# Pool caches handed over transposed, and a 64-token sample tile in retention

## The chip, the cores and the metric

The kernel runs on one core of a Trainium2 chip. The metric is the device time of one execution in microseconds (us), lower is better. TensorE is called PE below, VectorE DVE, ScalarE ACT, GpSimd POOL and SyncE SP.

## The reference

Two layers, each a mixer and a mixture of experts, on 512 prompt tokens and a sample group of 8 sequences with 8 new tokens each (64 tokens). All data is float32.

```
u, q, k, v, g = split(rmsnorm(x) @ w_in)                    # 512 columns each
pool: c = cumsum(concat([prev, u]))                         # prev: cache_pool, the last 15 rows of u of each sample sequence
      d = (c[t] - c[t - w]) / w - u                         # w = 2, 4, 8, 16 for the four groups of 128 channels
      y = d @ w_pool[group] * pool_scale
retention (4 heads of 128), in chunks:
      scores = (q @ k.T) * decay_mat
      o      = scores @ v + (q * q_decay) @ s
      o      = (o - mean(o)) * rsqrt(var(o) + eps);  ret_out = silu(g) * o
x += concat([pool_out, ret_out]) @ w_out
x += HierMoE(rmsnorm(x))                                    # 16 experts, two for each token
```

For the prompt the chunk is 128 tokens with a carried state; for the samples it is the 8 tokens of a sequence, with the state `state_ret` of that sequence.

## The kernel before

**Tiles of tokens.** Tokens lie in five tiles (`NT = 5`): tiles 0 to 3 are the prompt, the last (`LAST = 4`) holds the 64 sample tokens (`NSAMP`) in its first 64 rows. `tokens(t)` is 128 for a prompt tile and 64 for the last.

**Large products.** Each float32 product is made of float32r matmuls of a high and a low part of both factors (lines L464 to L468, 512 columns each): ACT makes the high part of a 256 KB piece of weights (`wh`), DVE the low part (`wl`), SP loads the pieces into `raw`. The input product runs over 40 such steps (`WIN_STEPS`: five groups of 512 columns, eight steps each), the output product over 16 more (`wout_mm`).

**What is put between the steps.** The order on every engine is written out by hand. After some input steps PE does a piece of pooling or retention: at steps `U_AT = (9, 13, 17, 21)` it turns `u` of one channel group so that channels are on partitions (five transposes of a 128x128 tile, L1744 and L1745), and with a sixth (L1746) the pool caches of the samples, `cpn`, 120 rows of which (8 sequences of 15) were loaded token by token. ACT copies the three pieces into `uT` (`pool_u`, L1175 to L1177), POOL adds shifted copies of it (`window`, L842), DVE makes `dT` (`pool_d`, L2187 to L2193), and PE multiplies it by `wpool` (`pool_mix`, L1364) at steps `M_AT = (12, 16, 20, 25)`. POOL also does the rotary embedding (`rotate`, L822 to L825) between the windows.

**Retention.** For each tile `qk_t` transposes q and k, `scores` multiplies them (L1630), DVE multiplies the result by the decay (`score_decay`, L2235) into `scT`, and `outputs` (L1645, L1647, L1651) makes the outputs and the state of prompt tiles. The last tile goes through `scores` too, but its outputs are made by `sample_head`, transposed: a matmul of v with `scT` (L1663) and, for each sequence, one of its state with its 8 queries (L1665). ACT copies these four heads into `scT[1]`, `back` transposes them (L1696), and from there the last tile is treated as the others: `group_stats`, `group_root`, `group_norm`, `gated`, and `on_t`, which transposes the normed outputs for the output product (L1373). `sample_head`, `back` and `on_t` stand between steps of the output product.

**Then** come the router, a gather of the tokens of each expert by indirect DMA (L857, `hg<-xn_d,rowidx`), 16 experts, a scatter and the sums, and the next layer. `idle_turns` (L1410) are matmuls of zeros that only keep PE busy.

Of the kernel before, what the change touches and what calls it, by code (L numbers as in the profile page):

```python
# [18 lines left out]
ALU = mybir.AluOpType  # L19
ACT = mybir.ActivationFunctionType  # L20
# [7 lines left out]
P = 128  # L28
D = 1024
SEQ, DECB, DECS, PAST = 512, 8, 8, 4096  # L30
NL = 2
# [99 lines left out]
def build(nc, a, o):  # L131
# [6 lines left out]
    with ctx:  # L138
# [9 lines left out]
        def tile(name, shape, dt=F32, off=None):  # L148
            size = int(np.prod(shape[1:])) * (2 if dt == BF16 else 4)
            return nc.alloc_sbuf_tensor_at(name, shape, dt, offset=place(size) if off is None else off)  # L150
# [7 lines left out]
        pscale = tile("pscale", [P, NH])  # L158
        gn_at = place(4096)
        gnrow = tile("gnrow", [P, PW], off=gn_at)  # L160
        cpn = tile("cpn", [DECB * BUF, PW], off=gn_at + 2048)
        wr = tile("wr", [P, KC, 20])
        gcol = tile("gcol", [P, 2, NL, KC])
        rbias = tile("rbias", [P, 20])
# [199 lines left out]
        def c(name, *shape):  # L364
            v = cst[:, at[name][0]:at[name][1]]
            if len(shape) == 1:
                return v.rearrange("p (a b) -> p a b", a=shape[0])
            if len(shape) == 2:
                return v.rearrange("p (a b c) -> p a b c", a=shape[0], b=shape[1])
            return v  # L370
# [6 lines left out]
        def zq(t, name):  # L377
            return z[:, t, OFFS[name], :]

        def heads(ap):  # L380
            return ap.rearrange("p (h d) -> p h d", h=NH)
# [22 lines left out]
        def tokens(t):  # L404
            return NSAMP if t == LAST else P
# [178 lines left out]
        def _(sp):  # L584
# [60 lines left out]
            def pool_tables(L):  # L645
                if L:
                    sp.wait_ge(comb, COMBS * L)
                sp.dma_start(cpn[:, :], a["cache_pool"][L].rearrange("b r c -> (b r) c")).then_inc(small_ld, 16)
                sp.dma_start(wpool[:, :, :], a["w_pool"][L]).then_inc(small_ld, 16)
                sp.dma_start(pscale[:, :], a["pool_scale"][L]).then_inc(small_ld, 16)  # L650

# [316 lines left out]
        def _(sc):  # L968
# [200 lines left out]
            def pool_u(L, g):  # L1169

                if g or L:
                    sc.wait_ge(d_done, NH * L + g)
                sc.wait_ge(ut_done, NH * L + g + 1)
                samp = uT[:, 16 + SEQ:].rearrange("p (b w) -> p b w", b=DECB)
                sc.activation(uT[:, 16:16 + SEQ], ps[6][:, :], ACT.Copy).then_inc(uT_done, 1)  # L1175
                sc.activation(samp[:, :, 16:24], ps[7][:, 0:NSAMP].rearrange("p (b s) -> p b s", b=DECB), ACT.Copy).then_inc(uT_done, 1)
                sc.activation(samp[:, :, 1:16], ps[7][:, P:P + DECB * BUF].rearrange("p (b s) -> p b s", b=DECB), ACT.Copy).then_inc(uT_done, 1)  # L1177

            def pool_hi(L, g):

# [24 lines left out]

            def group_root(L, t):
                sc.wait_ge(gn_st, NT * L + t + 1)
                sc.activation(gnrt[:, :], mv[:, :, 1], ACT.Sqrt, bias=eps[:, 1:2], scale=1.0).then_inc(gn_rt, 1)

            def first_hi(k):  # L1210
                raw_there(sc, 0, k)
# [5 lines left out]
            for L in range(NL):  # L1217
# [50 lines left out]
                sc.wait_ge(st_ready, LAST * (L + 1))  # L1268
                sc.dma_start(o["new_ret_prompt"][L], st[:, :, :]).then_inc(st_st, 16)
                sc.wait_ge(o_mm, NT * (L + 1))  # L1270
                sc.activation(scT[1][:, :, :], heads(ps[B_OT][:, :]), ACT.Copy).then_inc(o_ev, 1)
                w_hi(L, WIN_STEPS + 8)
                o_hi(sc, L, 0)
                o_hi(sc, L, 1)
# [92 lines left out]
        def on_t(pe, L, t):  # L1367

            pe.wait_ge(on_done, NT * L + t + 1)
            if t >= 2:  # L1370
                pe.wait_ge(olo, NT * L + t - 1)
            for h in range(NH):
                last = pe.transpose(ps[B_ON[t % 2]][:, h * P:(h + 1) * P], on[t][:, h, :], ident)  # L1373
            last.then_inc(on_tr, 1)

# [1 line left out]
        def _(pe):  # L1378
# [245 lines left out]
            def scores(L, t):  # L1624

                T = NT * L + t
                pe.wait_ge(qk_ev, 2 * T + 2)
                pe.wait_ge(qd_done, T + 1)
                for h in range(NH):
                    last = pe.matmul(ps[B_SC][:, h * P:(h + 1) * P], kT[:, h, :], qT[:, h, :], start=True, stop=True)  # L1630
                last.then_inc(sc_mm, 1)

            def outputs(L, t):
# [20 lines left out]
            def sample_head(L, h):  # L1654

                if h == 0:
                    pe.wait_ge(sc_ev, NT * (L + 1))
                    pe.wait_ge(kd_done, NT * (L + 1))
                    for t in (2, 3, LAST):
                        z_there(pe, L, 4, t)  # L1660
                pe.wait_ge(s0_ld[h], 16 * (L + 1))
                out = ps[B_OT][:, h * P:(h + 1) * P]
                pe.matmul(out, zq(LAST, "v")[:, h * P:(h + 1) * P], scT[0][:, h, :], start=True, stop=False)  # L1663
                for b in range(DECB):
                    last = pe.matmul(out[:, b * DECS:(b + 1) * DECS], s0[h][:, b, :], qdT[0][:, h, b * DECS:(b + 1) * DECS],  # L1665
                                     start=False, stop=(b == DECB - 1))
                if h == NH - 1:
                    last.then_inc(o_mm, 1)
# [23 lines left out]
            def back(L):  # L1692

                pe.wait_ge(o_ev, L + 1)
                for h in range(NH):
                    last = pe.transpose(ps[B_OT][:, h * P:(h + 1) * P], scT[1][:, h, :], ident)  # L1696
                last.then_inc(o_back, 1)

            def own_rows(t):
# [16 lines left out]
            for L in range(NL):  # L1716
# [12 lines left out]
                for s in range(EARLY[L], WIN_STEPS):  # L1729
                    if L == 0 and s < KC:  # L1730
                        first_block(s)
                    else:
                        for t in range(NT):
                            win_mm(L, s, t)
                    if s in U_AT:
                        g = U_AT.index(s)
                        if g == 0:
                            for t in range(NT):
                                z_there(pe, L, 0, t)
                            pe.wait_ge(small_ld, 96 * L + 64)  # L1740
                        else:
                            pe.wait_ge(plo, 8 * L + 2 * g)
                        for t in range(LAST):
                            pe.transpose(ps[6][:, t * P:(t + 1) * P], unat[:, t, g * P:(g + 1) * P], ident)  # L1744
                        pe.transpose(ps[7][:, 0:P], unat[:, LAST, g * P:(g + 1) * P], ident)  # L1745
                        pe.transpose(ps[7][:, P:P + DECB * BUF], cpn[:, g * P:(g + 1) * P], ident[0:DECB * BUF, 0:DECB * BUF]).then_inc(ut_done, 1)  # L1746
                    if s in M_AT:
                        pool_mix(pe, L, M_AT.index(s))
                    if s in T_AT:
                        qk_t(L, T_AT.index(s))  # L1750
                    if s in S_AT:
                        scores(L, S_AT.index(s))
                    if s in O_AT:
                        outputs(L, O_AT.index(s))
# [235 lines left out]
        def _(ve):  # L1990
            chain = [0]

            def link(ins):

                chain[0] += 1
                ins.then_inc(dve_chain, 1)
                ve.wait_ge(dve_chain, chain[0])
# [233 lines left out]
            def score_decay(L, t):  # L2231

                T = NT * L + t
                ve.wait_ge(sc_mm, T + 1)
                ve.tensor_tensor(scT[t % 2][:, :, :], heads(ps[B_SC][:, :]), c("decay", 2, NH)[:, int(t == LAST), :, :], ALU.mult).then_inc(sc_ev, 1)  # L2235

            def o_bank(t):
                return ps[B_O if t < LAST else B_OT]

            def group_stats(L, t):  # L2240

                if t < LAST:
                    ve.wait_ge(o_mm, NT * L + t + 1)
                else:
                    ve.wait_ge(o_back, L + 1)
                for h in range(NH):
                    last = ve.bn_stats(bnst[:, h, :], o_bank(t)[:, h * P:(h + 1) * P])
                link(last)
                for h in range(NH):
                    last = ve.bn_aggr(mv[:, h, :], bnst[:, h, :])  # L2250
                last.then_inc(gn_st, 1)

            def state(L, t):
# [13 lines left out]
            def group_norm(L, t):  # L2267

                T = NT * L + t
                ve.wait_ge(gn_rt, T + 1)  # L2270
                link(ve.reciprocal(gnrs[:, :], gnrt[:, :]))
                for h in range(NH):
                    last = ve.tensor_scalar(on[t][:, h, :], o_bank(t)[:, h * P:(h + 1) * P], mv[:, h, 0:1], gnrs[:, h:h + 1], ALU.subtract, ALU.mult)
                last.then_inc(gn_free, 1)

            def gated(L, t):

                T = NT * L + t
                ve.wait_ge(gn_free, T + 1)
                ve.wait_ge(sg_done, T + 1)  # L2280
                ve.tensor_tensor(on[t][:, :, :], on[t][:, :, :], heads(zq(t, "g")), ALU.mult).then_inc(on_done, 1)

            def sample_state(L, h):

# [189 lines left out]
```

## Time and profile before

| | |
|---|---|
| median of 3 runs | 837.12 us (836.44 to 838.64) |
| the profiled execution | 837.1 us, its span 835.1 us |
| busy share of the span | PE 97%, PE weight loads 79%, DVE 72%, ACT 58%, POOL 38% |
| mean granted clock of TensorE | 0.995 |

The span runs from the first to the last instruction. Times inside the span count from its start: layer 0 has its mixer up to about 235 us and its experts up to 400, layer 1 its mixer up to 646 and its experts up to 810. A busy PE is not a PE at its peak, so the rows are read by when the next instruction starts, and not by how long one lasts.

### The profile page before, as it was taken

The numbers are of one execution on the slowest core, as the hardware profiler recorded it, in microseconds if no ns is written. First come the engines' busy times: TensorE is split into PE (matmuls) and PEld (weight loads), VectorE is DVE, ScalarE is ACT, GpSimd is POOL, SyncE is SP. The second block draws the span as 40 slices with busy tenths as digits, with TensorE's granted clock in tenths as the row PEclk, the third lists the DMA queues.
The fourth block names the chain that finished last, engine by engine and source line by source line (L and its number), as shares of the span: only waits on it lengthen the run. The fifth ranks groups of instructions, "written<-read, shape, count | busy, mean of one in ns | idle before, by whom it ended". The sixth has DMA issues, their size and how long they took to land.

```text
span 835.1 us, 11973 instructions
## 1 busy us (share of the span) xinstructions
PE 814.2 (97%) x4104; PEld 656.6 (79%) x4104; DVE 599.4 (72%) x957; ACT 483.6 (58%) x824; POOL 315.4 (38%) x205
## 2 busy tenths in 40 slices
PE   9999999999999999999899999999999999999994
PEld 6887788888867888888488788888878578888861
DVE  5444654645689999999744454656647899999986
ACT  5533342612478888887653433353333898888874
POOL 0016991301041345664100199803101423665540
PEclk9999999999999999999999999999999999999998
DMA  9832223223939999998753222322278599999968
GB/s 323 271 109 76 72 57 98 91 70 137 411 128 361 388 355 377 397 368 300 255 185 92 85 76 64 87 64 78 78 263 346 179 417 360 383 378 391 344 219 280
DMA packets 57422, 188.17 MB, mean 225 GB/s; under 512 B 10877, under 2 KB 11645, under 8 KB 49163
## 3 DMA queue, kind: packets, MB, share of 16 engines
q1 hardware_dynamic: 44314, 156.55, 52.2%
q0 software_dynamic: 10368, 23.09, 7.4%
q10 hardware_dynamic: 2688, 7.88, 2.5%
q8 instruction: 29, 0.48, 0.2%
q14 instruction: 23, 0.18, 0.1%
HBM read 173.00 MB, written 29.39 MB: 242 GB/s over the span
## 4 chain that ended last, share of the span: by engine, by line
PE 71%; DVE 16%; DMA 5%; issue 4%; ACT 2%; DVEq 0%; ACTq 0%; POOLq 0%
PE ps L464 14%; PE ps L468 11%; PE ps L467 11%; PE ps L1414 5%; PE ps L1416 5%; PE ps L1415 5%; DVE gul L2110 4%; DVE dnl L2115 3%; PE ps L466 3%; PE ps L1422 2%; DVE hgTl L2126 2%; DMA y_d<-y,rowidx 2%; PE ps L1665 2%; DMA back<-y_d 1%; PE ps L1605 1%
## 5 line engine op out<-in xcount | busy, mean ns | idle before, releaser
L464 PE MATMUL ps<-wh,hT 128*128 128x512 f32 x472 | 189.4, 401 | 0.8 <-DVE wl L2101 0.4
L866 POOL DMA_INDIRECT y_d<-y,rowidx x32 | 116.4, 3638 | 124.1 <-DVE y L2135 124.1
L2110 DVE TENSOR_TENSOR gul<-wgu,eh 128x1024 fp32r<-128x1024 f32 x128 | 150.4, 1215 | 0.5 <-ACT eh L1105 0.5
L468 PE MATMUL ps<-wh,lT 128*128 128x512 f32 x377 | 147.2, 390 | 0.0
L467 PE MATMUL ps<-wl,hT 128*128 128x512 f32 x377 | 147.0, 390 | 0.0
L1105 ACT ACTIVATE eh<-wgu 128x1024 fp32r<-128x1024 f32 x128 | 128.4, 1058 | 3.7 <-PE ps L1416 3.7
L2101 DVE SCALAR_TENSOR_TENSOR wl<-raw,gcol,wh 128x512 fp32r<-128x512 f32 x80 | 75.3, 946 | 67.9 <-ACT wh L1078 67.8
L464 PEld LDWEIGHTS ps<-wh,hT 128*128 128x128 f32 x472 | 88.8, 188 | 18.8 <-issue 1.7
L1414 PE MATMUL ps<-eh,hgTh 128*128 128x512 f32 x240 | 96.4, 401 | 0.4 <-issue 0.4
L1416 PE MATMUL ps<-eh,hgTl 128*128 128x512 f32 x240 | 93.8, 391 | 0.0
L1415 PE MATMUL ps<-gul,hgTh 128*128 128x512 f32 x240 | 93.5, 390 | 0.0
L1078 ACT ACTIVATE wh<-raw,gcol 128x512 fp32r<-128x512 f32 x80 | 57.5, 721 | 57.9 <-PE ps L466 53.2
L468 PEld LDWEIGHTS ps<-wh,lT 128*128 128x128 f32 x377 | 70.8, 188 | 15.2
L467 PEld LDWEIGHTS ps<-wl,hT 128*128 128x128 f32 x377 | 71.0, 188 | 12.9
L2115 DVE TENSOR_TENSOR dnl<-wdn,eh 128x1024 fp32r<-128x1024 f32 x64 | 75.3, 1214 | 1.8 <-ACT eh L1118 1.7
L1118 ACT ACTIVATE eh<-wdn 128x1024 fp32r<-128x1024 f32 x64 | 64.5, 1061 | 0.0
L842 POOL TENSOR_TENSOR winA<-uT 128x719 f32<-128x719 f32 x8 | 11.1, 1387 | 115.3 <-ACT uT L1177 115.1
L857 POOL DMA_INDIRECT hg<-xn_d,rowidx x32 | 37.9, 1184 | 44.0 <-PE ps L1422 35.1
L1416 PEld LDWEIGHTS ps<-eh,hgTl 128*128 128x128 f32 x240 | 45.0, 188 | 9.9
L1414 PEld LDWEIGHTS ps<-eh,hgTh 128*128 128x128 f32 x240 | 45.1, 188 | 9.2 <-issue 0.8
L1415 PEld LDWEIGHTS ps<-gul,hgTh 128*128 128x128 f32 x240 | 45.2, 188 | 8.5
L1414 PE MATMUL ps<-eh,actTh 128*128 128x512 f32 x120 | 49.5, 413 | 0.0
(259 smaller groups left out, 1555.6 us busy)
## 6 DMA issues: line engine op xcount, KB each, us to landing
wgu<-in_gate_up SPq DMA_DIRECT2D x64, 1024.0 KB, 12.6
wdn<-in_w_down SPq DMA_DIRECT2D x64, 512.0 KB, 12.2
raw<-in_w_in SPq DMA_DIRECT2D x79, 256.0 KB, 2.7
raw<-in_w_out SPq DMA_DIRECT2D x32, 256.0 KB, 3.0
back<-y_d SPq DMA_DIRECT2D x16, 512.0 KB, 5.9
s<-in_state_ret POOLq DMA_DIRECT2D x8, 512.0 KB, 4.3
xn_d<-xf ACTq DMA_DIRECT2D x8, 512.0 KB, 6.2
x_in<-in_x_cols SPq DMA_DIRECT2D x8, 288.0 KB, 5.0
```

The lines of the kernel that those rows point to most:

```text
L464: pe.matmul(out, both, w_h, start=first, stop=False)
L467: pe.matmul(out, both, w_l, start=False, stop=False)
L468: return pe.matmul(out, l[:, t * P:(t + 1) * P], w_h, start=False, stop=final)
L866: pool.indirect_dma_start(out=y_d, out_offset=bass.IndirectOffsetOnAxis(ap=rowidx[:, 1, e:e + 1], axis=0), in_=y[s][:, :], in_offset=None, ...
L1105: sc.activation(gu_split(e, p)[:, :], gu_pair(wgu, wgu3, e, s, p), ACT.Copy).then_inc(ghi, 1)
L1118: sc.activation(dn_split(e, k)[:, :], dn_chunk(wdn, wdn3, e, s, k), ACT.Copy).then_inc(dhi, 1)
L1414: pe.matmul(out, hi_l, hi_r, start=first, stop=False)
L1415: pe.matmul(out, hi_l, lo_r, start=False, stop=False)
L1416: return pe.matmul(out, lo_l, hi_r, start=False, stop=final)
L2101: ve.scalar_tensor_tensor(out=wl[S % SPL][:, :], in0=raw[S % RAW][:, :], scalar=gcol[:, 0, L, s % KC:s % KC + 1], in1=wh[S % SPL][:, :].bi ...
L2110: ve.tensor_tensor(gu_pair(gul, gul3, e, s, p), gu_pair(wgu, wgu3, e, s, p), gu_split(e, p)[:, :].bitcast(F32), ALU.subtract).then_inc(glo, 1)
L2115: ve.tensor_tensor(dn_chunk(dnl, dnl3, e, s, k), dn_chunk(wdn, wdn3, e, s, k), dn_split(e, k)[:, :].bitcast(F32), ALU.subtract).then_inc(d ...
```

## The change

The host lays the pool caches out as channel, group, row (`pool_cols`), and SP loads them into `cpT` in place of `cpn`. PE no longer transposes them; ACT copies them from `cpT` to `uT`, ahead of the two copies that wait for PE's transposes. The wait for the small tables (`small_ld`) moves from PE to ACT, save for the first on PE. For the last tile, scores, decay, outputs, statistics, norm, gate and both transposes are cut to 64 tokens.

```diff
-        cpn = tile("cpn", [DECB * BUF, PW], off=gn_at + 2048)
+        cpT = tile("cpT", [P, NH, DECB * BUF], off=gn_at + 2048)
...
-                sp.dma_start(cpn[:, :], a["cache_pool"][L].rearrange("b r c -> (b r) c")).then_inc(small_ld, 16)
+                sp.dma_start(cpT[:, :, :], a["pool_cols"][L]).then_inc(small_ld, 16)
...
                 if g or L:
                     sc.wait_ge(d_done, NH * L + g)
+                samp = uT[:, 16 + SEQ:].rearrange("p (b w) -> p b w", b=DECB)
+                sc.wait_ge(small_ld, 96 * L + 64)
+                sc.activation(samp[:, :, 1:16], cpT[:, g, :].rearrange("p (b s) -> p b s", b=DECB), ACT.Copy).then_inc(uT_done, 1)
                 sc.wait_ge(ut_done, NH * L + g + 1)
-                samp = uT[:, 16 + SEQ:].rearrange("p (b w) -> p b w", b=DECB)
                 sc.activation(uT[:, 16:16 + SEQ], ps[6][:, :], ACT.Copy).then_inc(uT_done, 1)
                 sc.activation(samp[:, :, 16:24], ps[7][:, 0:NSAMP].rearrange("p (b s) -> p b s", b=DECB), ACT.Copy).then_inc(uT_done, 1)
-                sc.activation(samp[:, :, 1:16], ps[7][:, P:P + DECB * BUF].rearrange("p (b s) -> p b s", b=DECB), ACT.Copy).then_inc(uT_done, 1)
...
-                sc.activation(scT[1][:, :, :], heads(ps[B_OT][:, :]), ACT.Copy).then_inc(o_ev, 1)
+                sc.activation(scT[1][:, :, 0:NSAMP], heads(ps[B_OT][:, :])[:, :, 0:NSAMP], ACT.Copy).then_inc(o_ev, 1)
...
+            n = tokens(t)
             for h in range(NH):
-                last = pe.transpose(ps[B_ON[t % 2]][:, h * P:(h + 1) * P], on[t][:, h, :], ident)
+                last = pe.transpose(ps[B_ON[t % 2]][:, h * P:h * P + n], on[t][0:n, h, :], ident[0:n, 0:n])
             last.then_inc(on_tr, 1)
...
+                n = tokens(t)
                 for h in range(NH):
-                    last = pe.matmul(ps[B_SC][:, h * P:(h + 1) * P], kT[:, h, :], qT[:, h, :], start=True, stop=True)
+                    last = pe.matmul(ps[B_SC][0:n, h * P:h * P + n], kT[:, h, 0:n], qT[:, h, 0:n], start=True, stop=True)
                 last.then_inc(sc_mm, 1)
...
-                out = ps[B_OT][:, h * P:(h + 1) * P]
-                pe.matmul(out, zq(LAST, "v")[:, h * P:(h + 1) * P], scT[0][:, h, :], start=True, stop=False)
+                out = ps[B_OT][:, h * P:h * P + NSAMP]
+                pe.matmul(out, zq(LAST, "v")[0:NSAMP, h * P:(h + 1) * P], scT[0][0:NSAMP, h, 0:NSAMP], start=True, stop=False)
...
-                    last = pe.transpose(ps[B_OT][:, h * P:(h + 1) * P], scT[1][:, h, :], ident)
+                    last = pe.transpose(ps[B_OT][0:NSAMP, h * P:(h + 1) * P], scT[1][:, h, 0:NSAMP], ident)
...
-                            pe.wait_ge(small_ld, 96 * L + 64)
+                            if L == 0:
+                                pe.wait_ge(small_ld, 64)
...
-                        pe.transpose(ps[7][:, 0:P], unat[:, LAST, g * P:(g + 1) * P], ident)
-                        pe.transpose(ps[7][:, P:P + DECB * BUF], cpn[:, g * P:(g + 1) * P], ident[0:DECB * BUF, 0:DECB * BUF]).then_inc(ut_done, 1)
+                        pe.transpose(ps[7][:, 0:P], unat[:, LAST, g * P:(g + 1) * P], ident).then_inc(ut_done, 1)
...
-                ve.tensor_tensor(scT[t % 2][:, :, :], heads(ps[B_SC][:, :]), c("decay", 2, NH)[:, int(t == LAST), :, :], ALU.mult).then_inc(sc_ev, 1)
+                n = tokens(t)
+                ve.tensor_tensor(scT[t % 2][0:n, :, 0:n], heads(ps[B_SC][:, :])[0:n, :, 0:n], c("decay", 2, NH)[0:n, int(t == LAST), :, 0:n],
+                                 ALU.mult).then_inc(sc_ev, 1)
...
-                ve.tensor_tensor(on[t][:, :, :], on[t][:, :, :], heads(zq(t, "g")), ALU.mult).then_inc(on_done, 1)
+                n = tokens(t)
+                ve.tensor_tensor(on[t][0:n, :, :], on[t][0:n, :, :], heads(zq(t, "g"))[0:n], ALU.mult).then_inc(on_done, 1)
...
+    caches = host["cache_pool"].reshape(NL, DECB * BUF, NH, P)
+    host["pool_cols"] = np.ascontiguousarray(caches.transpose(0, 3, 2, 1))
```

`group_stats`, `group_root` and `group_norm` are cut to the first 64 partitions in the same way; their instructions keep their number and their 128 elements in each partition.

On PE, after step 9 of the input product of layer 0 (and the same at the other seven places in `U_AT`), these rows stand; `cst` is the identity:

```order
 L464 MATMUL ps<-wh_61,hT 128x512
 L466 MATMUL ps<-wl_65,hT 128x512
-L1744 MATMUL ps<-cst,unat 128x128 x4
-L1745 MATMUL ps<-cst,unat 128x128
-L1746 MATMUL ps<-cst,cpn 128x120
+L1749 MATMUL ps<-cst,unat 128x128 x4
+L1750 MATMUL ps<-cst,unat 128x128
 L464 MATMUL ps<-wh_62,hT 128x512
 L467 MATMUL ps<-wl_66,hT 128x512
```

One of six transposes is gone; nothing else moves.

On ACT, at the first `pool_u` of layer 0, between steps of weights:

```order
 L1078 ACTIVATE wh_60<-raw_82,gcol 128x512 [waits wpe,raw_ld0]
-L1175 ACTIVATE uT<-ps 128x512 [waits ut_done]
-L1176 ACTIVATE uT<-ps 128x8x8
-L1177 ACTIVATE uT<-ps 128x8x15
+L1175 ACTIVATE uT<-cpT 128x8x15 [waits small_ld]
+L1177 ACTIVATE uT<-ps 128x512 [waits ut_done]
+L1178 ACTIVATE uT<-ps 128x8x8
 L1078 ACTIVATE wh_61<-raw_83,gcol 128x512 [waits wpe,raw_ld1]
```

The copy of the caches has moved ahead of the wait for PE, and two copies in place of three stand behind it.

On PE, the transposes of the normed outputs of the last tile (`on_211`), between steps 7 and 8 of the output product of layer 0:

```order
 L464 MATMUL ps<-wh_63,hP 128x512
 L466 MATMUL ps<-wl_67,hP 128x512
-L1373 MATMUL ps<-cst,on_211 128x128 x4
+L1376 MATMUL ps<-cst,on_211 128x64 x4
 L464 MATMUL ps<-wh_60,hT 128x512
 L467 MATMUL ps<-wl_64,hT 128x512
```

Their number and place stay; each has half the columns (the shape is that of the output). The same holds for the other narrowed matmuls.

## Rows read from the trace of the kernel before

**Rows 1.** The page: busy time, and the chain that ended last

```profile
PE 814.2 (97%) x4104; PEld 656.6 (79%) x4104; DVE 599.4 (72%) x957; ACT 483.6 (58%) x824; POOL 315.4 (38%) x205
...
PE 71%; DVE 16%; DMA 5%; issue 4%; ACT 2%; DVEq 0%; ACTq 0%; POOLq 0%
```

**Rows 2.** Waits of PE: total us, times, longest us

```profile
PE ps L1393 <- DVE x L2220: 2.1, 2, 1.6
...
PE ps L1364 <- DVE dT L2193: 0.2, 1, 0.2
```

**Rows 3.** Busy time by stretches: us, PE, PEld, DVE, ACT, POOL, clock, DMA

```profile
97.00:211.00 114.00, 114.00 (x637) 98.56 (x636) 60.67 (x145) 41.27 (x83) 42.14 (x38) 1.00 0.30 97
...
429.00:640.00 211.00, 210.20 (x1097) 176.92 (x1095) 112.35 (x222) 83.10 (x170) 74.64 (x61) 1.00 0.36 121
```

**Rows 4.** Weight loads by form: busy us, mean ns

```profile
L1630 PEld LDWEIGHTS ps<-qT,kT 128*128 128x128 f32 x80 | 10.5, 191 | 0.8
...
L1373 PEld LDWEIGHTS ps<-cst,on 128*128 128x128 f32 x40 | 4.7, 140 | 0.5
...
L1689 PEld LDWEIGHTS ps<-vb,kv_end 64*128 64x128 f32 x16 | 2.7, 186 | 4.9 <-issue 4.2 <-DVE y L2135 0.6
L1605 PEld LDWEIGHTS ps<-wr,xT 128*64 128x64 f32 x32 | 2.3, 141 | 0.7 <-issue 0.5
```

**Rows 5.** Timeline of weight loads after step 9: start us, us

```profile
38.68 0.14 PEld L1745 LDWEIGHTS ps<-cst,unat 128*128 128x128 f32 x1
38.79 0.14 PEld L1746 LDWEIGHTS ps<-cst,cpn 120*128 120x128 f32 x1
38.90 0.19 PEld L464 LDWEIGHTS ps<-wh,hT 128*128 128x128 f32 x1
```

**Rows 6.** Timeline of PE, the scores of the last tile, layer 0

```profile
162.29 1.06 PE L1630 MATMUL ps<-qT,kT 128*128 128x128 f32 x8
163.18 0.39 PE L1645 MATMUL ps<-z,scT 128*128 128x128 f32 x2
```

**Rows 7.** Timeline of weight loads, router logits of the last tile

```profile
235.30 0.54 PEld L1605 LDWEIGHTS ps<-wr,xT 128*64 128x64 f32 x8 [0.23 <-issue]
```

**Rows 8.** Timeline of PE at a pool product

```profile
48.59 1.02 PE L1364 MATMUL ps<-dT,wpool 128*128 128x512 f32 x2
49.45 0.33 PE L1365 MATMUL ps<-dT,wpool 128*128 128x64 f32 x2
```

**Rows 9.** Timeline of PE in `sample_head`, head 1

```profile
173.38 0.38 PE L1663 MATMUL ps<-scT,z 128*128 128x128 f32 x2
173.60 1.85 PE L1665 MATMUL ps<-qdT,s 128*128 128x8 f32 x16
175.31 0.48 PE L464 MATMUL ps<-wh,hP 128*128 128x512 f32 x1
```

**Rows 10.** Timeline of ACT at `pool_u`, group 3 of layer 0

```profile
82.86 0.60 ACT L1175 ACTIVATE uT<-ps 128x512 f32<-128x512 f32 x1 [2.42 <-PE ps L1746]
...
83.45 0.28 ACT L1177 ACTIVATE uT<-ps 128x120 f32<-128x120 f32 x1
```

**Rows 11.** Timelines of DVE, POOL and PE at that group's product

```profile
91.24 1.26 DVE L2187 TENSOR_TENSOR edge<-winB,cst 128x16 f32<-128x16 f32 x1
...
90.84 1.63 POOL L822 TENSOR_TENSOR ropA<-z,cst 128x512 f32<-128x512 f32 x1
...
95.10 0.39 PE L466 MATMUL ps<-wl,hT 128*128 128x512 f32 x1
95.71 1.12 PE L1364 MATMUL ps<-dT,wpool 128*128 128x512 f32 x2 [0.23 <-DVE dT L2193]
```

**Rows 12.** Stretch of layer 0 at half the clock, columns as rows 3

```profile
236.40:239.80 3.40, 3.40 (x18) 1.59 (x17) 2.40 (x11) 2.69 (x5) 2.16 (x3) 0.50 0.35 77
```

**Rows 13.** The chain from a first transpose to the gather, both layers

```profile
226.88 0.92 PE ps L1393 x8
...
243.38 4.41 DMA hg<-xn_d,rowidx
...
637.62 0.92 PE ps L1393 x8
...
653.33 4.43 DMA hg<-xn_d,rowidx
```

More of the change, by code:

```diff
@@ L1207, in group_root @@
                 sc.wait_ge(gn_st, NT * L + t + 1)
-                sc.activation(gnrt[:, :], mv[:, :, 1], ACT.Sqrt, bias=eps[:, 1:2], scale=1.0).then_inc(gn_rt, 1)
+                n = tokens(t)
+                sc.activation(gnrt[0:n, :], mv[0:n, :, 1], ACT.Sqrt, bias=eps[0:n, 1:2], scale=1.0).then_inc(gn_rt, 1)
             def first_hi(k):
@@ L2245, in group_stats @@
                     ve.wait_ge(o_back, L + 1)
+                n = tokens(t)
                 for h in range(NH):
-                    last = ve.bn_stats(bnst[:, h, :], o_bank(t)[:, h * P:(h + 1) * P])
+                    last = ve.bn_stats(bnst[0:n, h, :], o_bank(t)[0:n, h * P:(h + 1) * P])
                 link(last)
                 for h in range(NH):
-                    last = ve.bn_aggr(mv[:, h, :], bnst[:, h, :])
+                    last = ve.bn_aggr(mv[0:n, h, :], bnst[0:n, h, :])
                 last.then_inc(gn_st, 1)
@@ L2270, in group_norm @@
                 ve.wait_ge(gn_rt, T + 1)
-                link(ve.reciprocal(gnrs[:, :], gnrt[:, :]))
+                n = tokens(t)
+                link(ve.reciprocal(gnrs[0:n, :], gnrt[0:n, :]))
                 for h in range(NH):
-                    last = ve.tensor_scalar(on[t][:, h, :], o_bank(t)[:, h * P:(h + 1) * P], mv[:, h, 0:1], gnrs[:, h:h + 1], ALU.subtract, ALU.mult)
+                    last = ve.tensor_scalar(on[t][0:n, h, :], o_bank(t)[0:n, h * P:(h + 1) * P], mv[0:n, h, 0:1], gnrs[0:n, h:h + 1],
+                                            ALU.subtract, ALU.mult)
                 last.then_inc(gn_free, 1)
@@ L2280, in gated @@
                 ve.wait_ge(sg_done, T + 1)
-                ve.tensor_tensor(on[t][:, :, :], on[t][:, :, :], heads(zq(t, "g")), ALU.mult).then_inc(on_done, 1)
+                n = tokens(t)
+                ve.tensor_tensor(on[t][0:n, :, :], on[t][0:n, :, :], heads(zq(t, "g"))[0:n], ALU.mult).then_inc(on_done, 1)
             def sample_state(L, h):
```

## The prediction

> **What bounds the kernel now.** I read the page first: PE is busy 97% of the span and holds 71% of the chain that ended last, DVE 16% [rows 1]. The list of PE's waits comes next, since busy time is no proof: the longest entry is 2.1 us in all, at the start of layer 1, and the only one inside a mixer's middle part is 0.2 us before a pool product [rows 2]. Then the stretches of the mixers: from 97 to 211 us PE is busy 114.00 of 114.00 us, from 429 to 640 us 210.20 of 211.00, at the full clock, while DVE, ACT and POOL are idle about half the time or more and DMA is at 0.30 and 0.36 [rows 3]. So in the mixer each thing that PE does adds its own slot to the time, and a slot is the distance between starts, since neighbours overlap. Everything that the change removes or narrows on PE lies in these two mixers, so a slot saved should reach the end, if no other engine is late by as little as the slot.
>
> **What a slot costs.** Two things can set it, the load of the weights and the streaming of the other tile. Streaming: a pass of 512 float32 columns takes (49.45 - 48.59) / 2 = 0.43 us [rows 8], which is 0.84 ns a column, so 128 columns are 107 ns and 64 are 54. Weights of an ordinary float32 matmul: the 16 passes that stream only 8 columns still stand (175.31 - 173.60) / 16 = 107 ns apart [rows 9], so a load of 128 columns holds the array for at least 107 ns whatever is streamed. With 64 columns of weights, 8 loads last 0.54 us together, one alone 0.141: (0.54 - 0.14) / 7 = 57 ns each [rows 4, 7]. A load lasts 191 ns with 128 columns and 141 with 64 [rows 4]. In a transpose the load of a full 128 columns lasts 140 ns [rows 4], as long as the half-width ordinary one, so I take it to hold the array for only some 57 ns; the transposes' slot of 109 ns (38.79 to 38.90) [rows 5] then comes from streaming the identity.
>
> **The change, part by part.**
>
> The cache transposes: eight are removed, four in a layer, at 109 ns from one load to the next [rows 5]. 8 x 0.109 = 0.87 us. This is the surest term; each stands alone in a dense row of PE.
>
> The scores of the last tile: 4 matmuls, 8 passes, in each layer, (163.18 - 162.29) / 8 = 111 ns a pass [rows 6]. Weights and stream are both halved: 57 ns by the load, 54 by the stream, so 57. 16 x 0.054 = 0.86 us.
>
> `on_t` of the last tile: 8 transposes. Weights stay 128 columns wide (64 rows), the identity shrinks to 64 columns: from 109 to about 57 ns, 8 x 0.052 = 0.42 us. The price hangs on the reading of the 140 ns load. Bounds: 0 if the load were the limit after all, 0.44 if streaming alone counted (8 x 0.055).
>
> `back`: 8 transposes whose weights shrink to 64 columns while the whole identity is streamed, 107 ns as before. I take 0; the upper bound is 8 x 0.052 = 0.42 us.
>
> The v matmul of `sample_head`: 8 matmuls, 16 passes; the stream shrinks to 64 columns, the weights keep 128 columns and lose only rows. The passes of 8 columns beside them stand at 107 ns [rows 9], and a load with 64 rows and 128 columns lasts 186 ns against 191 with 128 rows [rows 4]. I take 0; the upper bound is 16 x 0.054 = 0.86 us.
>
> [...]
>
> ACT: the copy of the caches (0.28 us) moves ahead of the wait for PE. ACT stands idle 2.42 us there [rows 10], so the copy lies in idle time, and `uT` is complete about 0.1 us (copy) + 0.11 us (transpose) sooner. If that cover were gone the copy would cost 0.28 us eight times on ACT, which itself is idle half of the mixer, so nothing on PE. The wait for `small_ld` that ACT takes over cannot be later than before: PE made the same wait ahead of the transposes that ACT then waited for. What is queued behind it on ACT is the next high part of weights, with the same bound.
>
> DVE and ACT on the narrower tile: `score_decay` and the copy of the outputs lose half their elements, the others none; PE waits for neither [rows 2], so 0. The cache load has as many bytes for the same issue, so 0.
>
> What is late next: the one place where DVE holds PE up is the pool product of group 3 in layer 0, which starts 95.71 - 95.10 = 0.61 us after its forerunner instead of 0.23 us. There DVE's 16-element `edge` lasts 1.26 us, up to the end of POOL's `ropA` (90.84 + 1.63 = 92.47) [rows 11]. POOL's start and DVE's start both move with PE's, so I leave this wait as it is; 0.38 us could be won there.
>
> Sum: 0.87 + 0.86 + 0.42 = 2.15 us. The profiled execution took 837.1 us (835.1 us of span and 2.0 around it), the median of the runs is 837.12. 837.1 - 2.1 = **835.0 us**, 0.25% less. A measurement of this kernel can tell some 0.3% (2.5 us) from no change, so the likeliest case is just inside "no difference".
>
> **The rivals.**
>
> *Less is paid back* (836.1 us, 0.17). The weight load bounds transposes and half-width scores gain less: 0.87 us and little more arrives, 1.0 us in all. [...] Against it: the 57 ns loads. It too is "no difference".
>
> *All narrowing pays* (833.7 us, 0.13). `back` and `sample_head` gain as well: 2.15 + 0.42 + 0.86 = 3.4 us. Against it: the 107 ns of the 8-column passes.
>
> *The clock no longer falls before the experts* (834.2 us, 0.18). In layer 0 the granted clock is 0.50 (1.2 GHz) from 236.4 to 239.8 [rows 12], after PE has done short transposes and logits; in layer 1 the same work leaves it at 2.4 GHz. From the same transposes to the first gather layer 0 takes 243.38 - 226.88 = 16.50 us and layer 1 653.33 - 637.62 = 15.71 [rows 13]: the fall costs 0.8 us. The change brings this place 1.1 us forward in layer 0 and 2.1 in layer 1, so the fall may go (835.0 - 0.8 = 834.2), or come in layer 1 too (835.8, which is in the likeliest case's range).
>
> *POOL and DVE meet worse* (slower, 841 us, 0.06). `edge` shows that a short DVE operation can stand for the whole of a POOL operation. `uT` comes a little sooner in relation to DVE, so POOL's windows and rotations shift against `pool_d`. If each of its four operations for group 3 waited out one more POOL operation of 1.63 us, that is 6.5 us in a layer, of which PE would feel nearly all in layer 0, and most in layer 1. That gives 835.0 + 6 = 841. It decides once the added stall passes 2.1 + 2.5 = 4.6 us over both layers. Against it: the shift is only some 0.1 us, and groups 0 to 2 never held PE. [...]
>
> *The change does what it says, but elsewhere* is no case of its own: both mixers are bound by PE.
>
> **How the numbers follow.** The likeliest case, 2.15 us with 0.4 either way for the terms and 0.8 for the clock, has 0.46 (834.2 to 836.0). Faster by over 0.3%: all narrowing and the lost clock fall, with a little of the likeliest, 0.13 + 0.18 + 0.03 = 0.34. Slower: 0.05 of the POOL case. Within 0.3%: 0.61. The range of 8 in 10 takes in all narrowing at its low end with a little of the clock, and no gain at its upper end, since the runs shown differ by 2.2 us: 833.0 to 837.0.
>
> **What would show it.** In the profile after: five transposes of `unat` at each of the eight places, and L464 right behind them; the 8 score passes of the last tile about 57 ns apart (0.45 us in place of 0.89); `on_t` of the last tile about 57 ns apart; `back` still near 108; the v passes of `sample_head` still near 110. The distance from the first pool transposes to the first logits should shrink by 1.07 us in each layer. The prediction is wrong if `on_t` stays at 109, if v passes fall to 57, if PE's waits before the pool products grow from 0.2 us, or if the stretch at 0.50 goes or doubles.

## The result, and the profile after

The changed kernel took 848.07 us (median of 6 runs, 844.59 to 851.20) against 836.78 us (6 runs, 835.88 to 839.19) of the kernel before: a ratio of 1.0133, with a 95% interval of 1.0118 to 1.0149. It is slower by 11 us, where 2 us less had been forecast. Its runs also lie further apart, 6.6 us against 3.3 us.

The page of the changed kernel, busy time, the granted clock in 40 slices and the chain that ended last, as in [rows 1]:

```profile
PE 827.3 (98%) x4096; PEld 662.0 (78%) x4096; DVE 600.1 (71%) x957; ACT 483.3 (57%) x824; POOL 315.5 (37%) x205
...
PEclk9999999989999999999999999999699999999998
...
PE 71%; DVE 17%; DMA 5%; issue 4%; ACT 2%; DVEq 0%; POOLq 0%; ACTq 0%
```

PE has eight instructions fewer and is busy 13 us longer. The busy time of DVE, ACT and POOL differs by less than 1 us. The row of the clock says where to look: it has a dent at slice 9 (170 to 191 us) and a deep one at slice 29 (594 to 615 us). The waits of PE do not explain 11 us; this is their first row, and the row of the pool product that answers to [rows 2]:

```profile
PE ps L1396 <- DVE x L2224: 2.2, 2, 1.6
...
PE ps L1366 <- DVE dT L2197: 0.6, 2, 0.3
```

The stretches of the changed kernel around the dents (columns as in [rows 3]; the eighth column is the granted clock, 1.00 for full speed and 0.50 for half of it):

```profile
177.20:180.60 3.40, 3.40 (x24) 2.85 (x24) 3.26 (x5) 1.05 (x3) 0.00 (x0) 1.00 0.43 143
180.60:184.00 3.40, 3.40 (x10) 2.65 (x9) 1.90 (x3) 0.63 (x1) 0.00 (x0) 0.50 0.66 181
184.00:187.50 3.50, 3.50 (x25) 2.95 (x24) 0.00 (x0) 0.22 (x1) 0.00 (x0) 0.99 0.17 60
187.50:190.90 3.40, 3.40 (x10) 2.63 (x9) 0.69 (x1) 0.69 (x2) 0.00 (x0) 0.51 0.19 64
...
586.80:590.20 3.40, 3.40 (x10) 2.36 (x8) 0.00 (x0) 0.00 (x0) 0.00 (x0) 0.50 0.00 0
...
593.60:603.90 10.30, 10.30 (x34) 8.38 (x33) 5.16 (x8) 2.19 (x4) 0.00 (x0) 0.50 0.40 127
...
607.30:610.70 3.40, 3.40 (x9) 2.66 (x9) 0.69 (x1) 0.82 (x2) 0.00 (x0) 0.50 0.18 55
```

PE is "busy" all the time in each of them. The stretch from 180.60 to 184.00, at 0.50, holds large matmuls alone, 10 of them; at the full clock's 0.23 us apiece it would be 14 or 15. (The 24 and 25 of the stretches at full clock have the 18 short passes of a head in them.) In the mixers of this execution the clock is at 0.50 for 3.4 + 3.4 us in layer 0 and 3.4 + 10.2 + 3.4 us in layer 1, 24 us in all. I call each such stretch a fall. The kernel before has 1.00 from 97 to 211 and from 429 to 640 [rows 3].

The loss arises where the falls are. Matched matmul by matmul with the kernel before, the output product's matmul that started at 155.8 us starts 0.1 us earlier in the changed kernel, the one of 195.8 us starts 4.4 us later; in layer 1 it is 4.4 us at 566.6 and 13.6 us at 606.5. Between the two pairs lie the four heads of `sample_head` of each layer.

The timeline of PE in the changed kernel shows what stands right before a fall, and how the large matmuls slow down in it:

```profile
177.47 0.39 PE L466 MATMUL ps<-wl,hP 128*128 128x512 f32 x1
177.79 0.43 PE L1667 MATMUL ps<-scT,z 64*128 64x64 f32 x2
178.16 1.95 PE L1669 MATMUL ps<-qdT,s 128*128 128x8 f32 x16
179.96 0.48 PE L464 MATMUL ps<-wh,hP 128*128 128x512 f32 x1
...
181.25 0.63 PE L467 MATMUL ps<-wl,hP 128*128 128x512 f32 x1
181.68 0.63 PE L468 MATMUL ps<-wh,lP 128*128 128x512 f32 x1
```

A head of `sample_head` precedes the fall, as it does each of the other four, and from 181.25 the large matmuls start 0.43 us apart, where it was 0.23. The head itself has become longer: from L466 to L464 it is 179.96 - 177.47 = 2.49 us, against 0.23 + (175.31 - 173.38) = 2.16 us before [rows 9]. The v product, now 64*128, starts 0.32 us after the matmul ahead of it instead of 0.23, and its two passes last to 178.16, 0.37 us, instead of 0.22, although each streams half as many columns. The weight loads at the head ahead of that one show what is different, first in the kernel before and then in the changed one:

```profile
172.93 0.19 PEld L468 LDWEIGHTS ps<-wh,lP 128*128 128x128 f32 x1
173.16 0.41 PEld L1663 LDWEIGHTS ps<-scT,z 128*128 128x128 f32 x2
...
173.06 0.19 PEld L468 LDWEIGHTS ps<-wh,lP 128*128 128x128 f32 x1
173.60 0.29 PEld L1667 LDWEIGHTS ps<-scT,z 64*128 64x128 f32 x2 [0.35 <-issue]
173.97 0.63 PEld L1669 LDWEIGHTS ps<-qdT,s 128*128 128x128 f32 x5
```

The load of 128 rows began 0.23 us after the load ahead of it, 0.22 us before its own matmul (173.38 [rows 9]). The load of 64 rows begins 0.54 us after the load ahead of it and only 0.01 us before its own matmul starts (173.61): it is not done under the running matmul any more. The full load behind it, at 173.97, starts together with its own matmul too. "issue" says that the engine waited for nothing that the profile shows; why the load isn't made earlier, no run here shows.

For each group of small matmuls I took the distance from the start of the large matmul ahead of it to the start of the second large one behind it, where both are at the full clock, in both traces (ns; groups as in the source):

```
group                               times   before   after   difference
u and cache transposes                8      1120     1011      -108
scores, last tile (with outputs 3)    2      4040     3942       -98
sample_head, one head                 8      2466     2802      +336
back and on_t 0, 1                    2      1771     1771         0
on_t, last tile                       2       900     1046      +146
pool product, group 3, layer 0        1      2031     2108       +77
pool product, group 3, layer 1        1      1548     2115      +567
```

The sum is -0.86 - 0.20 + 2.69 + 0 + 0.29 + 0.64 = +2.6 us before any fall of the clock. (Of the eight heads five are read at the full clock and differ by 335 to 336; the 336 is taken for the other three.) The profiled executions are 850.35 - 837.1 = 13.3 us apart, which leaves 10.7 us. The falls account for it: in 24 us at half the clock large matmuls stand 0.43 us apart and not 0.23, which loses 24 x (1 - 0.23 / 0.43) = 11.2 us; the fall at 236 us, 0.8 us in the prediction's reckoning, is missing in this execution, where the clock is 1.00 from 229 to 247. What is left, some 0.3 us, is no more than what arises between the layers (0.6 us). The six runs bear it out: the mean granted clock sinks from 0.989 in the fastest (844.59 us) to 0.981 in the slowest (851.20), with 0.983 and 0.985 between.

### The profile page after: what moved, and what is told of

Read it like the earlier page. It is cut to its first block, busy times and chain, and to the rows that moved or that the text cites. A ratio compares the mean times of both kernels' runs of the same rounds, so it can differ in the third digit from the quotient of the medians.

```text
span 848.5 us, 11956 instructions
## 1 busy us (share of the span) xinstructions
PE 827.3 (98%) x4096; PEld 662.0 (78%) x4096; DVE 600.1 (71%) x957; ACT 483.3 (57%) x824; POOL 315.5 (37%) x205
## 4 chain that ended last, share of the span: by engine, by line
PE 71%; DVE 17%; DMA 5%; issue 4%; ACT 2%; DVEq 0%; POOLq 0%; ACTq 0%
PE ps L464 14%; PE ps L467 11%; PE ps L468 11%; PE ps L1417 5%; PE ps L1419 5%; PE ps L1418 5%; DVE gul L2114 4%; DVE dnl L2119 3%; PE ps L466 3%; PE ps L1669 2%; PE ps L1425 2%; DVE hgTl L2130 2%; DMA y_d<-y,rowidx 2%; DMA back<-y_d 1%; PE ps L1608 1%
## 5 line engine op out<-in xcount | busy, mean ns | idle before, releaser
L464 PE MATMUL ps<-wh,hT 128*128 128x512 f32 x472 | 189.5, 401 | 0.9 <-DVE wl L2105 0.4
L464 PEld LDWEIGHTS ps<-wh,hT 128*128 128x128 f32 x472 | 88.8, 188 | 19.4 <-issue 1.7
L2108 DVE TENSOR_TENSOR wl<-raw,wh 128x512 fp32r<-128x512 f32 x32 | 22.8, 718 | 42.6 <-ACT wh L1080 42.6
```

The costliest lines, as they stand in the source:

```text
L464: pe.matmul(out, both, w_h, start=first, stop=False)
```

## The experiments

Theory A: loads of 64 rows are not made ahead, as that of the v product above (0.01 us before its own matmul in place of 0.22), which lengthens the stretch of thin work (passes that stream few columns) in `sample_head`, and this makes the granted clock fall. The rivals are the cache part with its new timing (B), streamed columns alone (C), the other narrowed matmuls (D), and stalls alone (E). Ratios are to the kernel before on the same chip, with 95% intervals.

**Only the caches** (the cache part of the change on the kernel before).

```diff
-                        pe.transpose(ps[7][:, P:P + DECB * BUF], cpn[:, g * P:(g + 1) * P], ident[0:DECB * BUF, 0:DECB * BUF]).then_inc(ut_done, 1)
+                sc.activation(samp[:, :, 1:16], cpT[:, g, :].rearrange("p (b s) -> p b s", b=DECB), ACT.Copy).then_inc(uT_done, 1)
```

> Only the cache part of the change: caches handed over transposed, eight PE transposes fewer, ACT's copy moved ahead; the last tile as wide as before. Theory A (partial-array matmuls of the narrowed tile stall, and the stretch that they thin out makes the granted clock fall): no fall of the clock in the mixers, PE saves 8 x 0.108 us, 0.2 us or so may be lost before the pool products, so 836.1 us. Theory B (the cache part, by its new timing of ACT, POOL and DVE, carries the loss): 840 us or more.

837.17 us, ratio 0.9996 (0.9984 to 1.0007). No fall in the mixers, so theory B is out. The eight distances shrink by 108 ns each as forecast, and the two pool products of group 3 grow by 79 and 561 ns; what is left, 0.2 us, is too little to measure.

**Only half the columns in the v product.**

```diff
-                out = ps[B_OT][:, h * P:(h + 1) * P]
-                pe.matmul(out, zq(LAST, "v")[:, h * P:(h + 1) * P], scT[0][:, h, :], start=True, stop=False)
+                out = ps[B_OT][:, h * P:h * P + NSAMP]
+                pe.matmul(out, zq(LAST, "v")[:, h * P:(h + 1) * P], scT[0][:, h, 0:NSAMP], start=True, stop=False)
```

> The kernel before, with only the v product of sample_head streaming 64 columns in place of 128; all 128 rows of its weights stay. The columns 64 to 127 of each head that ACT then copies are leftovers and belong to no token. Theory A: weights of full height are loaded ahead as before, the two passes stay near 108 and 110 ns, no time lost in the slots, 836.8 us; the clock falls at most seldom. Theory C (what counts for the clock is the streamed columns alone): 32 passes stream half as much, the clock falls in the mixers, 841 us or more.

837.17 us, ratio 1.0006 (0.9996 to 1.0017). Every head's distance is unchanged at 2466 ns: half the stream saves nothing here, which the prediction had, and does no harm either. The two v passes start 55 ns apart in place of 108, but the loads start as before (the second v load 227 ns behind the first, the next one 108 ns on), and the second 8-column pass stands 84 ns behind the first in place of 31: the 53 ns are gone again. Theory C is out as an account of this loss. It isn't shown that streamed columns count for nothing: this kernel takes 64 of them from each of 16 passes and adds no time, which is a much smaller change than 0.34 us more in each head.

**Only half the rows in the v product.**

```diff
-                pe.matmul(out, zq(LAST, "v")[:, h * P:(h + 1) * P], scT[0][:, h, :], start=True, stop=False)
+                pe.matmul(out, zq(LAST, "v")[0:NSAMP, h * P:(h + 1) * P], scT[0][0:NSAMP, h, :], start=True, stop=False)
```

> The kernel before, with only the v product of sample_head reading 64 rows of weights in place of 128; it still streams 128 columns. Theory A: each of the eight heads takes about 0.33 us longer (the weights of a half-height matmul are not loaded under a full one, nor the other way round), 2.7 us in all, and the clock falls in the stretch of sample_head as in the changed kernel: 843 to 848 us. Theory C: no fall and no loss, 836.8 us.

847.93 us (843.93 to 849.93), ratio 1.0118 (1.0082 to 1.0153). One slice of a matmul that computes the same outputs brings the whole loss. A head is 389 ns longer, a little more than in the changed kernel: with 128 streamed columns the two v passes start 213 ns apart, with 64 there 160. In the profiled execution 17 us of the mixers stand at 0.50. The stretches of this kernel around `sample_head`, in both layers:

```profile
165.00:211.00 46.00, 46.00 (x229) 37.67 (x228) 22.27 (x58) 9.28 (x18) 3.93 (x2) 0.89 0.22 63
575.00:621.00 46.00, 46.00 (x252) 38.41 (x251) 25.19 (x65) 10.48 (x22) 6.88 (x5) 0.93 0.16 51
```

**The changed kernel with v and scores at 128**, and the decay between them.

```diff
-                n = tokens(t)
...
-                    last = pe.matmul(ps[B_SC][0:n, h * P:h * P + n], kT[:, h, 0:n], qT[:, h, 0:n], start=True, stop=True)
+                    last = pe.matmul(ps[B_SC][:, h * P:(h + 1) * P], kT[:, h, :], qT[:, h, :], start=True, stop=True)
...
-                out = ps[B_OT][:, h * P:h * P + NSAMP]
-                pe.matmul(out, zq(LAST, "v")[0:NSAMP, h * P:(h + 1) * P], scT[0][0:NSAMP, h, 0:NSAMP], start=True, stop=False)
+                out = ps[B_OT][:, h * P:(h + 1) * P]
+                pe.matmul(out, zq(LAST, "v")[:, h * P:(h + 1) * P], scT[0][:, h, :], start=True, stop=False)
...
-                n = tokens(t)
-                ve.tensor_tensor(scT[t % 2][0:n, :, 0:n], heads(ps[B_SC][:, :])[0:n, :, 0:n], c("decay", 2, NH)[0:n, int(t == LAST), :, 0:n],
-                                 ALU.mult).then_inc(sc_ev, 1)
+                ve.tensor_tensor(scT[t % 2][:, :, :], heads(ps[B_SC][:, :]), c("decay", 2, NH)[:, int(t == LAST), :, :], ALU.mult).then_inc(sc_ev, 1)
```

> The changed kernel with scores, decay and the v product of sample_head back at 128; caches, back, norm, gate and on_t stay changed. Theory A: nothing narrow is left in the heads, no fall of the clock in the mixers; -0.87 us (caches), +0.29 us (on_t of 64 rows), some 0.6 us before the pool products: 836.8 us. Theory D (on_t and back, or the whole narrowing, make the clock fall): 841 us or more.

836.41 us, ratio 0.9994 (0.9982 to 1.0006), clock 1.00 in both stretches. `on_t` of 64 rows is still in it and costs its 146 ns, but no fall follows: theory D is out for `on_t` and `back`.

**The changed kernel with the v product tall again**, scores still narrow; DVE zeroes the unused half of them.

```diff
-                pe.matmul(out, zq(LAST, "v")[0:NSAMP, h * P:(h + 1) * P], scT[0][0:NSAMP, h, 0:NSAMP], start=True, stop=False)
+                pe.matmul(out, zq(LAST, "v")[:, h * P:(h + 1) * P], scT[0][:, h, 0:NSAMP], start=True, stop=False)
...
+                if t == LAST:
+                    ve.memset(scT[0][NSAMP:P, :, 0:NSAMP], 0.0)
```

> The changed kernel with one thing undone: the v product of sample_head reads 128 rows of weights again and streams 64 columns; rows 64 to 127 of the scores are set to zero by DVE ahead of the decay. Theory A: the half-height weights alone were the cause; no fall in the mixers, no added 0.33 us a head: -0.87 (caches) -0.19 (scores) +0.29 (on_t) +0.64 (pool products) = -0.1 us, 836.9 us. If scores, on_t and caches together also thin the stretch enough: 840 us or more.

836.01 us, ratio 0.9988 (0.9975 to 1.0002). All else of the change is in it, every head's distance is the 2466 ns of the kernel before again, and the 11 us are gone. The stretches of this kernel, with the clock at 1.00:

```profile
165.00:211.00 46.00, 46.00 (x252) 39.20 (x250) 23.69 (x58) 10.72 (x21) 3.92 (x2) 1.00 0.37 121
575.00:621.00 46.00, 46.00 (x253) 39.34 (x253) 23.64 (x60) 10.38 (x21) 3.92 (x2) 1.00 0.36 119
```

**The changed kernel, filled.** Two matmuls of zeros of 512 columns behind each head; they compute nothing.

```diff
                 if h == NH - 1:
                     last.then_inc(o_mm, 1)
+                idle_turns(4, 2)
```

> The changed kernel plus two matmuls of zeros of 512 columns behind each head of sample_head (16 in all, 0.217 us each: 3.5 us more work). If the falls of the clock carry most of the loss (theory A), this work makes the kernel faster than the changed one (848.1 us): fewer falls, 842 to 845 us. If the loss is in the slots and waits (theory E: stalls alone, the clock falling anyway), it is slower: 851 us.

845.20 us (843.65 to 847.41), ratio 1.0106 (1.0083 to 1.0130). Its median is 2.9 us below that of the changed kernel (848.07) with 2.8 us more work in it, though the intervals of the two ratios overlap (up to 1.0130 here, from 1.0118 there). In the profiled execution (843.65 us, the fastest of the four) no mixer stretch is below 1.00, and the large matmuls of layer 1's experts come 4.7 us later than before: 8 x 0.68 = 5.4 us for the heads with their filling, -0.1 us for the rest of the table above, and some 0.8 us back for the fall at 236 us, which it doesn't have. (The rest, up to 843.65 - 837.1 = 6.6 us, comes behind the last expert, where the kernel waits for scattered rows.) The filling doesn't take the falls away for good: the runs of 846.49 and 847.41 us have a mean granted clock of 0.988 and 0.989, against 0.993 in the profiled one, and so they probably hold some. Stalls alone (E) asked for 851 us, and the interval ends at 847.7: E is out.

**The kernel before, thinned**: behind each v product (and so within the head, where the expectation says behind it) two more matmuls of 8 columns into a spare bank, four passes of full height.

```diff
+                for _ in range(2):
+                    pe.matmul(ps[4][:, 0:DECS], s0[h][:, 0, :], qdT[0][:, h, 0:DECS], start=True, stop=True)
```

> The kernel before plus, behind each head of sample_head, two copies of its first 8-column matmul into a spare bank (four passes of full height, 0.11 us each: 0.45 us a head, 3.6 us in all). No partial matmul is in it. Theory A in its general form (the clock falls where the thin stretch grows longer, whatever makes it longer): falls in the mixers as in the changed kernel, 846 us or more. If the falls need partial-height matmuls: 840.4 us.

848.51 us, ratio 1.0129 (1.0110 to 1.0148). A head is 446 ns longer, 3.6 us in all; the other 8 us come with the falls, 20 us at 0.50 in the mixers of the profiled execution, and no matmul of the heads has fewer than 128 rows or columns of weights. Around `sample_head` this kernel shows:

```profile
168.40:171.80 3.40, 3.40 (x28) 3.23 (x27) 1.72 (x4) 0.00 (x0) 0.00 (x0) 1.00 0.00 0
171.80:175.20 3.40, 3.40 (x10) 2.66 (x9) 0.00 (x0) 0.00 (x0) 0.00 (x0) 0.50 0.00 0
...
595.00:605.20 10.20, 10.20 (x36) 8.95 (x35) 5.16 (x8) 2.23 (x4) 0.00 (x0) 0.50 0.42 129
```

**The kernel before, filled**, its twin with dense work: `idle_turns(4, 2)` behind each head, as above.

> The kernel before plus the same two matmuls of zeros of 512 columns behind each head as in the filled version of the changed kernel: 3.5 us of dense work. It is the twin of the thin version. Theory A: no falls, 840.3 us. If any added PE time in this stretch upsets the clock: 844 us or more.

841.06 us, ratio 1.0056 (1.0034 to 1.0079). A head is 345 ns longer, 2.8 us in all, and in the profiled execution no mixer stretch is below the full clock. (One of its four runs, 843.70 us, has a mean clock of 0.990 against 0.994 to 0.997, and may hold a fall.) Of the 4.1 us that its profiled execution (841.22) lies above the one before, 1.8 us arise between the layers, half of them because the scatter of the last rows landed after 5.16 us instead of 4.24; I take that for a matter of the execution. The changed kernel's heads are longer by the same 336 ns, with stalls and partial passes in them, and it loses 7 us more. So it matters here what fills the time.

**The kernel before, thinned by half**: one such copy, in the same place, instead of two.

> The kernel before plus one copy of the first 8-column matmul behind each head (two passes, 0.22 us a head, 1.8 us in all): half the dose of the thin version that ran at 848.5. If the clock falls by degree, some falls, 841 to 845 us; if the kernel before is far enough from the edge, none, 838.6 us.

839.16 us, ratio 1.0023 (1.0013 to 1.0033). A head is 0.23 us longer, which makes 1.9 us, and this is all that is seen; the stretches stand at the full clock:

```profile
165.00:211.00 46.00, 46.00 (x260) 39.81 (x260) 22.97 (x59) 10.29 (x20) 3.95 (x2) 1.00 0.32 103
575.00:621.00 46.00, 46.00 (x265) 39.98 (x264) 23.08 (x60) 9.92 (x19) 3.95 (x2) 1.00 0.30 94
```

The loss is not in proportion to what is added: 0.23 us of thin work more in each head cost nothing beyond themselves, while 0.34 (changed kernel), 0.39 (half rows) and 0.45 us (thinned) brought falls, and the times of these three, 848.07, 847.93 and 848.51 us, are alike.

**The caches alone, and the last pool product one step later.** The edit against the first experiment:

```diff
-U_AT, M_AT = (9, 13, 17, 21), (12, 16, 20, 25)
+U_AT, M_AT = (9, 13, 17, 21), (12, 16, 20, 26)
```

> The cache part alone, and the product of the last pool group one step of weights later (M_AT 26 in place of 25), so that DVE's late operations have 3.4 us more. If the wait before that product gives back 0.64 us of the 0.87 us that the removed transposes save, it goes: no wait before either product of group 3, 0.87 + 0.48 us less than before, 835.6 us. If the later place delays the transposes of q and k instead: 837 us or more.

835.44 us (835.04 to 837.19), ratio 0.9978 (0.9967 to 0.9989). This is the only version that is measurably faster than the kernel before, by 0.2%. PE no longer waits before a pool product, and the product's own distance is 1540 and 1542 ns in both layers.

## Why the prediction was wrong

The way to the number failed at two steps.

The first is the term of the v product: "I take 0; the upper bound is 16 x 0.054 = 0.86 us". Its lower bound was missing: I reasoned that a load of 64 rows takes as long as one of 128 (186 against 191 ns) and that nothing could change but the stream. The length of the load hardly changed, as I had read; its start did. The half-height load begins 0.01 us before its own matmul, where the full one began 0.22 us before it, and the full load behind it starts together with its own matmul too: +336 ns a head, 2.69 us in all. The same error sits in two other terms. `on_t` of the last tile was to save 0.42 us and costs 0.29: its passes do stand 62 to 65 ns apart, so the reading of the 140 ns load was about right, but the first load at either border, from full height to half and back, costs more than the three short distances give (the passes' starts follow one another by 320, 110, 62, 65 and 152 ns, from the matmul ahead to the one behind, where they were 233, 108, 108, 109 and 28). The scores were to save 0.86 us and save 0.20: passes 58 ns apart as forecast, less the same borders (their first load, too, begins 0.54 us after the load ahead of it). The rows held two warnings. The 64-row loads of L1689 stand in [rows 4] with 4.2 us of idle ahead of the 16, released by "issue", about 0.26 us each, where the 80 full loads of L1630 have 0.8 us together; the prediction uses only their length, 186 ns. The router's loads, 64 columns wide, have 0.23 us of the same kind ahead of them [rows 7], and it uses only the distance inside the group.

The second and larger is the sentence "So in the mixer each thing that PE does adds its own slot to the time", with the clock held at 1.00. The rival on the clock knew that a fall costs something, but placed it only before the experts, where [rows 12] show one, and expected mainly a gain. (It writes 1.2 and 2.4 GHz; the profiles show 0.50 and 1.00 of full speed, and no run shows a frequency.) What it named did happen in the profiled execution, which has no fall at 236 us (0.8 us back), and it was drowned by 24 us of falls elsewhere. That fall moves with small shifts: the first experiment has it at 236.7 us, the second has it at 647 us and the fourth nowhere. `sample_head` is the thinnest stretch of the mixer: 16 passes of 8 columns, on average 107 ns apart, 1.7 us in a row [rows 9]. The kernel before was within 0.34 us a head of falling there, and its rows, with the clock at 1.00, did not show it; the thinned version did. In size this step weighs more: the falls bring some 11 us of the profiled execution's loss, the other terms together cost 2.6 us where 2.15 us were to be saved.

What held: the caches (0.86 us against 0.87), `back` (0), columns alone in `sample_head` (0), ACT's copy and its wait (no wait of PE traces back to them). So did the reading of the shapes and of the two things that set a slot. In the changed kernel `back` is 8 matmuls in all, with 128*64 weights (`scT`, cut to 64 columns) and 128x128 streamed (the identity), and `on_t` of the last tile 8, with 64*128 and 64x64; each is one pass, while the 8 v products are 16. Streaming set the slot of the transposes: `back` loads half the columns and its passes stay 108 to 109 ns apart, `on_t` keeps its 128 columns of weights, streams 64, and goes from 109 to 62 and 65 behind its second pass. The load set it in `sample_head`: the pass behind the second v pass starts 110 ns after it whether that one streams 128 columns (the kernel before) or 64 (the second experiment), and the 8-column passes behind stand 111 to 112 ns apart. The wait before the pool products of group 3 was assumed to stay, and grew from 0.48 to 0.56 us in layer 0 and from nothing to 0.57 us in layer 1. The rival of POOL and DVE had the place and, as the timelines read, the long DVE operations beside POOL's, at a tenth of its size. In layer 1 `edge` already stood beside a whole `ropA` in the kernel before (1.25 us, up to 503.71 and 503.69); what is new there are the two last operations for `dT`, 1.27 and 1.33 us in place of 0.66 and 0.76, the last of which ends at 510.77, when POOL's L825 does (510.68). That POOL's operations hold DVE's up is my reading of these times; no run tests it. But this wait also changes without the change: the second and third experiments have it in layer 1 alone, the thinned kernels in layer 0 alone, the filled twin in neither. With the cache part it stands in both layers in four of the five kernels that keep the product's place, and in layer 1 alone in the fifth. So I don't count all of it to the change. With the product one step later it is gone.

What stays open: whether half-height matmuls also count less for the clock than full ones of the same length. The thinned version shows that they are not needed for a fall, and the half-dose version that 0.23 us more are harmless; between 0.23 and 0.34 us the runs don't separate length from height. Nor do they say what about the thin work counts, its columns or its time: no version streams fewer columns by as much without also taking longer.

## What to carry to other kernels

Cutting a matmul to its valid rows was no saving by itself here: the v product lost 336 ns in each head, the four transposes of `on_t` 146 ns, and only the eight passes of the scores, cut in columns, saved 98 ns. So compare the slot at the borders with full-size neighbours, and cut only where the distances, measured as above, show that the run of such matmuls pays for the way in and out; here zeros in the unused rows were cheaper than a slice (836.01 against 848.07 us). And before PE work is thinned or removed in a stretch that is already thin, test how far the clock is from falling by adding a little thin work there: this kernel, with the clock at 1.00 in that stretch, stood 0.23 us more in each of eight places without a fall, and lost more than a per cent with 0.34 us more.

## What the hardware showed that I had not expected

- A load of weights of 64 rows behind a matmul with 128 began 0.54 us after the load ahead of it, in place of 0.23 us, and a head with such a pair of passes took 0.34 us longer though it streamed half the columns. Weights of 128 rows and 64 columns (the scores) show the same at their borders: 8 passes 58 ns apart save only 98 ns as a group.
- The granted clock fell from 1.00 to 0.50 while PE was busy without a gap, 0.4 to 1.2 us after the last of 16 passes of 8 columns had started (five falls of the changed kernel). It fell again in neighbouring stretches, up to 10.2 us in a row; in that one lies a head that takes 5.2 us at half the clock in place of 2.8.
- Heads longer by 2.8 us in all through matmuls of zeros left the kernel at 841 us, heads longer by 3.6 us through 8-column matmuls put it at 848.5.
